# A gated linear recurrence with its projections as three rounded products, values and output gates of all heads first

## The reference, cut to what matters

```
def hg_dir(p, z, lb):
    q = jax.nn.silu(to_heads(p[4], HG_HEADS))
    lbh = lb.reshape(1, HG_HEADS, 1, HG_DK)
    f = lbh + (1.0 - lbh) * jax.nn.sigmoid(to_heads(z, HG_HEADS).astype(jnp.float32))
    return q, 1.0 - f, to_heads(p[7], HG_HEADS), jnp.log(f)
...
out = (jnp.einsum('bhts,bhsv->bhtv', scores, vc)
       + jnp.einsum('bhtd,bhdv->bhtv', qc * jnp.exp(b), state))
new_state = (jnp.exp(b_end[:, :, 0, :])[..., None] * state
             + jnp.einsum('bhsd,bhsv->bhdv', kc * jnp.exp(b_end - b), vc))
...
b = from_heads(rms_norm(o_hg, hg_norm_w_l)) * jax.nn.silu(p[8])
```

## Time and profile before

| what | value |
|---|---|
| runs | 2823.1, 2820.17, 2821.18 us; median 2821.18 |
| profiled execution, time | 2818.32 us |
| profiled execution, span | 2816.7 us, mean granted clock 0.978 |
| PE busy over the span | 2651.4 us, 94% |
| DVE, ACT, POOL busy over the span | 2079.2, 1426.4, 543.3 us |
| `hgrn2`, first uT scaling to last PE work | 48.6 to 555.5 us of the span |
| first `scores` of heads 0, 1, 2, 3 | 151.4, 266.0, 382.2, 498.4 us |

### The profile page before, as it was taken

The page is one execution under the profiler, slowest core; times in us unless marked ns, Lnnn a source line. Parts: engine busy times, 40 slices in busy tenths (PEclk is TensorE's granted clock), DMA queues, the critical chain, the costliest instruction groups (busy, mean ns, idle before and its releaser), DMA issues. The chain is left out here.

```text
span 2816.7 us, 43469 instructions
## 1 busy us (share of the span) xinstructions
PE 2651.4 (94%) x15273; PEld 2208.2 (78%) x15274; DVE 2079.2 (74%) x2433; ACT 1426.4 (51%) x1442; POOL 543.3 (19%) x437
## 2 busy tenths in 40 slices
PE   7899999899798899999999999999999999999994
PEld 3668577577687779777887978899989897888783
DVE  4566676673666796999879787866686778967884
ACT  4433535331634574777647565544454546645653
POOL 0524434200013211222121111111121112111110
PEclk9999999999899899999999999999999999999997
DMA  7101100180353796999969787866586769967864
GB/s 260 31 23 31 30 24 16 49 289 1 118 137 124 289 381 218 367 354 351 320 221 363 259 294 262 283 203 205 192 293 207 256 235 329 326 207 272 300 227 134
DMA packets 266663, 596.96 MB, mean 212 GB/s; under 512 B 21373, under 2 KB 47141, under 8 KB 265473
## 3 DMA queue, kind: packets, MB, share of 16 engines
q1 hardware_dynamic: 246208, 552.82, 54.9%
q0 software_dynamic: 20384, 43.19, 6.9%
HBM read 578.01 MB, written 42.25 MB: 220 GB/s over the span
## 5 line engine op out<-in xcount | busy, mean ns | idle before, releaser
L2100 ACT ACTIVATE whi<-e_slot 128x2048 fp32r<-128x2048 f32 x296 | 560.9, 1912 | 437.2 <-PE e_acc L2026 370.8
L2162 DVE TENSOR_TENSOR e_slot_r<-e_slot,whi 128x2048 fp32r<-128x2048 f32 x296 | 674.9, 2287 | 101.1 <-ACT whi L2100 101.1
L2023 PE MATMUL e_acc<-e_xhi,whi 128*128 128x256 f32 x1664 | 399.4, 282 | 3.2 <-ACT e_xhi L2104 3.2
L2100 ACT ACTIVATE whi<-slot 128x2048 fp32r<-128x2048 f32 x148 | 283.3, 1914 | 192.1 <-PE e_acc L1998 192.1
L2162 DVE TENSOR_TENSOR slot_r<-slot,whi 128x2048 fp32r<-128x2048 f32 x151 | 344.7, 2285 | 19.7 <-ACT whi L2100 16.7
L1996 PE MATMUL e_acc<-whi,e_ahi 128*128 128x512 f32 x800 | 319.4, 399 | 0.0
L2023 PEld LDWEIGHTS e_acc<-e_xhi,whi 128*128 128x128 f32 x1664 | 313.1, 188 | 6.3 <-ACT e_xhi L2104 6.3
L1940 POOL DMA_INDIRECT sum<-yo,e_idx_now x50 | 122.3, 2446 | 1012.3 <-issue 539.4
L1998 PE MATMUL e_acc<-whi,e_alo 128*128 128x512 f32 x800 | 313.4, 392 | 0.0
L1997 PE MATMUL e_acc<-e_slot_r,e_ahi 128*128 128x512 f32 x800 | 311.6, 389 | 0.0
L1996 PE MATMUL e_acc<-whi,e_xhi 128*128 128x512 f32 x768 | 303.3, 395 | 0.8 <-DVE e_slot_r L2162 0.5
(11 more groups left out here) (338 smaller groups left out, 4794.8 us busy)
## 6 DMA issues: line engine op xcount, KB each, us to landing
e_slot<-in_w SPq DMA_DIRECT2D x296, 1024.0 KB, 7.1
slot<-in_w SPq DMA_DIRECT2D x151, 1024.0 KB, 7.3
rv<-in_w_ada SPq DMA_DIRECT2D x32, 512.0 KB, 4.7
slot<-in_w_in SPq DMA_DIRECT2D x20, 512.0 KB, 4.1
wa<-in_w_ada SPq DMA_DIRECT2D x8, 1024.0 KB, 17.1
slot<-in_w_in SPq DMA_DIRECT2D x6, 1024.0 KB, 8.6
xt<-in_x SPq DMA_DIRECT2D x8, 512.0 KB, 14.7
slot<-in_w_out SPq DMA_DIRECT2D x4, 1024.0 KB, 13.0
```

What stands on the lines that cost most here:

```text
L2023: pe.matmul(out[:, c, :], whi[i % RING][:, w], xhi[:, kk, :], start=first, stop=False, skip_group_check=True)
L2100: act.activation(whi[i % RING][:], raw[i % PIECES][:], ACT.Copy).then_inc(S["whi_made"], 1)
L2162: v.tensor_tensor(wlo[i % PIECES][:], raw[i % PIECES][:], whi[i % RING][:].bitcast(F32), ALU.subtract).then_inc(S["wlo_made"], 1)
```

## The change

1. The rounding of `uT` into `uhi` and a remainder moves from `project_retention` to the start of `hgrn2` (`high_rows`, `low_rows`). All projections of the recurrence, and `early_rows`, are now three float32r products.
2. The values of all four heads are projected first, tile by tile at width 512 (ten groups of 24 products), copied out and stored to DRAM (`hg_values`); each head loads its part again (`load_values`).
3. Then come the six z groups and two query groups of head 0, then the output gates of all heads in two pairs at width 256 (16 groups of 24 products), also through DRAM (`hg_gates`). Between them stand the transposes and updates of head 0.
4. Per head the loop now holds z and queries alone. Each head's three weight chunks are rounded on ACT (`high_chunk`, 128x1024) and DVE (`low_chunk`); for the chunks of the next head's z, DVE does this between the first and the second `pick`; for the queries' weights, between the second running sum and the last `pick`.
5. The last two z groups of a head stand behind the first and the second `scores` of the second half (`z_order`). Keys and running sums have one buffer each, no longer two.
6. ACT does the two key decays directly behind the logarithms, ahead of the first query sigmoid and the roots. The gate's sigmoid is one ACT step on 1024 columns a head, its two products are on POOL.
7. Backward keys in token order are written over `kdec0`; the output is written over the gate.

The core of the diff:

```diff
+            def turned_products(h, i, chunk, a, z):
...
+                for k in range(KT):
+                    pe.matmul(out, hi[:, k, :], uhi[:, k, a:z], start=(k == 0), stop=False)
+                    pe.matmul(out, lo[:, k, :], uhi[:, k, a:z], start=False, stop=False)
+                    mm = pe.matmul(out, hi[:, k, :], ulo[:, k, a:z], start=False, stop=(k == KT - 1))
...
+            values(0, (0, 1))
+            values(1, (0, 1))
+            values(0, (2,))
+            values(1, (2,))
+            for x in range(2, NT):
+                values(x, (0, 1, 2))
+            for i in range(6):
+                gates_of_keys(0, i)
+            queries(0, 0)
+            queries(0, 1)
+            for x in range(6):
+                output_gates(x)
+            turn_keys(0, 0)
+            turn_keys(0, 1)
...
+            updates(0)
+            for x in range(12, 2 * LT):
+                output_gates(x)
+            for h in range(HEADS):
+                more = h + 1 < HEADS
+                for j in range(HT):
+                    scores(h, j)
+                    if j:
+                        output(h, j - 1)
+                if more:
+                    gates_of_keys(h + 1, 0)
...
+                output(h, HT - 1)
+                if more:
+                    for i in range(1, 4):
+                        gates_of_keys(h + 1, i)
...
+                for j in range(HT, LT):
+                    scores(h, j)
+                    if j > HT:
+                        output(h, j - 1)
+                    if more and j < HT + 2:
+                        gates_of_keys(h + 1, 4 + j - HT)
+                if more:
+                    queries(h + 1, 0)
...
+                output(h, LT - 1)
...
+                if more:
+                    queries(h + 1, 1)
+                    for n in range(6):
+                        turn_keys(h + 1, n)
+                    updates(h + 1)
```

DVE's loop:

```diff
                 if now:
-                    for j in range(HT):
+                    pick(h, 0)
+                    if more:
+                        low_chunk(3 * h + 3)
+                        low_chunk(3 * h + 4)
+                    else:
+                        low_early(0)
+                        low_early(1)
+                    for j in range(1, HT):
                         pick(h, j)
                     finish(h, 0)
                     levels(h, 1)
...
                 if more:
                     cumulate(h + 1, 1)
+                    if now:
+                        low_chunk(3 * h + 5)
                 if now:
                     pick(h, HT + 3)
```

More of the change, by code:

```diff
@@ L222, in _ @@
                     load_x(i)
-            for n in range(len(keep["h_W"])):
+            for half in range(2):
+                load_value_weights(sp, dram, keep, half)
+            for n in range(2):
                 load_recurrence_weights(sp, dram, keep, n)
@@ L577, in output @@
                 mm.then_inc(S["o_done"], 1)
-            for h in range(-1, HEADS):
-                now, more = h >= 0, h + 1 < HEADS
-                if now:
-                    for j in range(HT):
-                        scores(h, j)
-                        if j:
-                            output(h, j - 1)
+            values(0, (0, 1))
[4 more added lines that the diff above has]
+                values(x, (0, 1, 2))
@@ L707, in _ @@
+            for i in range(6):
+                copy_z(0, i)
+                if i == 4:
+                    high_chunk(2)
             act.wait_ge(S["eps_set"], 1)
             act.wait_ge(S["bounds"], 3)
-            for h in range(-1, HEADS):
-                now, more = h >= 0, h + 1 < HEADS
+            logs(0)
+            query_sig(0, 0)
+            query_sig(0, 1)
+            key_decays(0)
+            output_gate(0)
+            output_gate(1)
+            query_decays(0)
+            output_gate(2)
@@ new lines, in _ @@
+            output_gate(3)
+            high_gates(1)
+            output_gate(4)
+            output_gate(5)
+            turned_keys(0, 0)
+            turned_keys(0, 1)
+            for n in range(2, 6):
+                output_gate(4 + n)
+                turned_keys(0, n)
+                levels(0, 0, (n - 2,))
+            for x in range(10, 2 * LT):
+                output_gate(x)
+                if x < 12:
+                    levels(0, 0, ((4,), (5, 6))[x - 10])
+            high_chunk(3)
@@ L711, in _ @@
+            high_chunk(4)
+            gate_sig(0)
+            for h in range(HEADS):
+                more = h + 1 < HEADS
+                if h and more:
+                    high_chunk(3 * h + 3)
+                    high_chunk(3 * h + 4)
+                if not more:
+                    high_early(0)
+                    high_early(1)
                 if more:
                     copy_z(h + 1, 0)
-                if now:
-                    roots(h, 0)
-                    levels(h, 1, range(0, 2))
+                roots(h, 0)
+                levels(h, 1, range(0, 2))
@@ L913, in _ @@
                     decayed(h + 1, 3)
+                    if not now:
+                        low_gates(1)
                     levels(h + 1, 0)
-                    gates(h + 1, 0)
                     states(h + 1)
-                    gates(h + 1, 1)
 ROW_JOBS = [O_RQ, O_RV, O_RG]
```

582 lines of the change are left out of this document (354 added, 228 removed).

## The result

The changed kernel takes 2908.11 us (median of 4 runs, 2902.44 to 2910.67), beside 2820.68 us for the kernel before on the same chip (4 runs). The ratio is 1.0306, with a 95% interval of 1.0288 to 1.0324: 87 us slower. The forecast was 65 us slower, 2885, in a range of 2848 to 2914.

A forecast was written before the change was run, and what follows sets the result against it. PE bound the loop before; after, the chain from engine to engine would. Start 61.6, three heads 5.5, last head 3.0 and join -4.8 made 65.3 us on 2818.3, so 2883.6; with the median 2.9 higher it said 2885, range 2848 to 2914.

The forecast's parts named there:

- What PE saves: PE's projections in the recurrence: 253.2 us against 307.5, early rows 21.8 against 27.5, so 60 us less work.
- rival (a): PE stays the bound, links overlap, a head takes PE's 73 us: 2753 us; chance 0.05.
- (b): Shorter chain, still slower: clock back at once, exponents keep up with POOL; head 110.6 us, total 2864 or 2855; chance 0.17.
- (d): It evens out, within 5 us of the kernel before: a head of about 96 us; chance 0.03.
- The start: Everything ahead of head 0's first scores: they come at 213, 61.6 us later than before.
- The chain: Engine-to-engine links from one head's first scores to the next's: 113 us, 117.5 with the clock, against 116.2 before.
- The levels: Link from POOL's 28 subtractions through DVE's multiplies, behind a head's first scores: 25.9 us, not shortened by the change.
- The last head: Head 3, with two 128x2048 halves rounded on DVE between the first two picks: 60.1 us, 3.0 more than before.
- The join: PE's 7.3 us wait between the recurrence and the next stage, for roundings now already done: 4.8 us off.
- The moved decays: ACT's key decays done earlier in a head: costed at nothing, covered by the 29 us of levels.
- The sum: Start 61.6, three heads 5.5, last head 3.0, join -4.8: 65.3 us slower than the kernel before.
- rival (c): Longer chain: half clock behind about six waits a head, DVE and POOL colliding; 2909 to 2915, or 2924; chance 0.15.

The follow-up runs named there:

- e4: The kernel before with its values and output gates cut to the first of their eight matmuls, so both are wrong: 2760.49 us.
- e2: The changed kernel with the first four z groups of heads 1 to 3 cut to the first of their three products: 2902.97 us.
- e8: The changed kernel with matmuls of no use put into four waits of PE, writing a bank that nothing reads: 2901.34 us.
- e1: The changed kernel with ACT's key decays of heads 1 to 3 put back behind the query sigmoid and the roots: 2905.66 us.
- e5: The changed kernel with the last two z groups ahead of the second half's scores, and DVE's states moved between the level multiplies: 2857.84 us.
- e11: The kernel before with only ACT's key decays moved ahead of the query sigmoid and roots, and DVE's two multiplies by them moved up: 2819.75 us.
- e7: e5 with DVE's roundings of weights also moved to where DVE waits: 2846.10 us.
- e9: e7 with five edits at waits: earlier key-decay multiplies and states, later POOL gate products, head 0's roundings put back, own banks for its queries: 2831.43 us.
- e10: e9 with 16 and 24 matmuls of no use ahead of the last updates and the first scores in heads 1 to 3: 2832.69 us.

## Why the prediction was right, point by point

**What PE saves.** Right as to the products, which run at the pitch of the earlier trace rows where PE has not waited; PE is busy for 79 to 82 us of a head in place of 111.5. I had said 73 us and 65%; it is 64 to 68%. Over the recurrence PE is busy for 445.6 us in place of 476.9, 31 us less and not 60, since matmuls behind waits last longer at the lower clock. e4 shows that a head of the kernel before waited for its values and gates for 7 us only, and e2 that a head of the changed kernel doesn't wait for the first four z groups at all; the last two z groups and the first query group do stand on its chain. This settles rival (a), 2753: not so. Rivals (b) and (d), a head of 110.6 or 96, are out by the windows. The Trainium skill (Perfetto Trace Analysis, Identifying the Most-Contended Engine) says to optimise the engine with the highest occupancy first; for TensorE it takes the share of matmul time as a poor measure of what is left to gain and names that of weight loads, which is 78% here and still above the other engines. By that rule PE was the place to work, and the trace of e4 agrees for the first 7 us of a head and no further.

**The start.** Right to 2.3 us: 215.3 for 213. The value groups end at 109.4 (110 said), and the first gate group starts at 157.1 behind a wait of 9.12 us for the query banks (157 and 9 said). The 2.3 us lie behind that: 58.2 us from there to the first scores, where the sum has 55.9.

**The chain.** Right in kind and in its links. Its size was 4 us a head too small (121.6 on average for 117.5), and this is the step that was mis-sized: "At 1.6 for a short one I take 2.2 each, bounds 0 and 3.5. The head comes to 113 + 4.4 = 117.5 us". The three links in which PE works behind a wait are 2.6, 2.1 and 2.4 us longer than forecast at full clock, 7.1 together in head 1, in place of 4.4, and 8.3 in head 2. For the first two e8 shows that it is the clock: filling the waits gives back 2.8 and 1.6 us in head 1. For the third the rows show it: the query group's first nine products stand some 0.43 us apart in place of 0.23. I had counted two waits ahead of groups and had left out the first scores, which stand behind the states: 3.7 us a tile there in place of 2.0. The levels were 1.7 us shorter than said in head 1 and as said in head 2.

**Head 0** takes 3.2 us more than head 1. Of these 1.9 are its levels, which came out in the longer of two ways as in head 2 (last section). The other 1.2 I had not seen: its two roundings for head 1's z wait for ACT and for weights that land late, and the second pick stands behind them (224.91 in the timeline of the changed kernel, 7 us behind the first). Its first scores have no wait ahead of them and run at 2.0 us a tile, so that its first link, 16.7 us for 12.8, is too long by these weights first; the clock adds its part only behind them, where PE has waited 4.17 us for the second pick and the fourth scores are slow.

**The last head** took 64.1 for 60.1. From its first scores to the second half's it takes 44.8 us, against 36.6 before: 4.5 for the roundings, as said, and 3.7 more, for which the slow scores are the likeliest cause (3.7 us for each of the first two tiles in place of 2.0, and a fourth pick that waits 2.66 us for scores, 0.46 before); that part was not tried apart.

**The join** gave 4.7 for 4.8.

**The moved decays** were costed at nothing; e1 makes it a gain of 0.6 us a head. The reason given, the cover of the levels, holds: DVE starts on the levels 2.3 us sooner, and 1.7 of these are lost again within them.

**The sum**: 65.3 said, 84.1 measured on the profiled execution: +2.3 start, +12.3 three heads, +4.0 last head, +0.1 join. The median, 2908.1, stands between the 2885 said (the sum and its 2.9 for the median make 2886.5) and rival (c). Of that rival's two mechanisms the first is seen, slow matmuls behind more waits than I had counted; that DVE and POOL hold each other up is seen too, but in head 1, where they do it most in the levels, these are shorter than said.

## What to carry to other kernels

Before work is taken off the busiest engine, walk the chain of one iteration: as long as the order stays, its length is the floor, and the distance to it (7 us of 116 here) is all that work taken from beside it can give, while work that moves ahead of the loop is paid in full. When the chain is the bound, look at the order on each queue: two groups moved ahead of two scores were worth 49 us, and no instruction was saved. A step that is made ready earlier helps only if the next engine's queue takes it up earlier too (e1, e5 and e11).

## What the runs showed of the hardware that I had not expected

The same 28 subtractions on POOL and 22 multiplies on DVE, in the same order, come out in two ways. In head 2 of the changed kernel DVE's first step takes 8.12 us, until POOL is through; in head 1 DVE gets in (0.93 us for the same step, 0.83 in place of 0.41 for the next) and POOL's pairs take 1.8 in place of 1.2. Both rows:

```profile
362.62 0.93 DVE L1058 TENSOR_TENSOR h_wk<-h_key,h_key 128x512 f32<-128x512 f32 x1
...
482.16 8.12 DVE L1058 TENSOR_TENSOR h_wk<-h_key,h_key 128x512 f32<-128x512 f32 x1
```

From POOL's first subtraction to DVE's last multiply it is 26.0 us the one way and 24.2 the other, which makes most of the difference between heads of 122.4 and 119.6 us. e1, e2, e5, e7 and e8 have the short way too, each in other heads, so single heads of two runs can be compared only where both went the same way. What decides between them stays open.

Filled waits bring the granted clock back (0.79 to 0.93 over a head), but in head 1 of e9 and of e10 a clock of 0.85 and of 0.88 makes 98.5 us alike: in these runs the clock had a price only where PE's work itself ended the next engine's wait.
